# Neighbourhood attention of an encoder block: query tiles by column half, two heads at a time

## The chip, the cores and the metric

The kernel runs on one core of a Trainium2 chip. The metric is the device time of one launch in microseconds; of the kernel before three runs gave 1609.84 to 1613.71, median 1612.07. All inputs and weights are float32 and come from HBM (274.6 MB move in one launch). TensorE's granted clock has two levels here, 2.4 GHz (1.00 in the profile) and 1.2 GHz (0.50).

## The reference, cut to what matters

One encoder layer on 16 meta tokens and 256 tokens (a grid of 4 rows by 64 columns), width 2048. The normalised tokens give q, k, v (16 heads of 64), the input u of a state-space branch and two gates. The part that changes is the attention:

```python
def neighbourhood_attention(q, k, v, rpb):     # rows = 4, kr = min(8, rows) = 4: every grid row is in reach
    col_start = jnp.clip(c_idx - COL_WIN // 2, 0, GRID_W - COL_WIN)          # 16 of 64 columns around the query
    ...
    s_loc = einsum('bchd,bicjhd->bhcij', q_r, k_win) * scale + bias           # 4 rows x 16 columns of keys
    s_meta = einsum('bchd,bmhd->bhcm', q_r, km) * scale                       # and the 16 meta tokens
    p = softmax(concatenate([s_loc, s_meta], axis=-1), axis=-1)
    return einsum(p_loc, v_win) + einsum(p_meta, vm)
```

A query in columns 0 to 31 reaches keys in columns 0 to 39 only, one in columns 32 to 63 keys in columns 24 to 63. Meta queries attend to the meta tokens. Behind it: y_na = attention @ w_proj_na; the state-space branch with GELU and a GLU (w_glu) and w_proj_ssm; both gated, @ w_out, residual; then a gated MLP with a convolution (w_up, w_down) and a last norm.

## The kernel before, in words

**Dense products.** Every weight matrix comes in units of 4 x 128 rows by 256 columns (512 KB) through four ring slots. SyncE's queue loads a unit (`load`, L360); ScalarE rounds it to `w_hi` (`hi_unit`, L426 to L430); GpSimd, in the first stages VectorE, makes the rest `w_lo` (`lo_unit`, L432 to L434); TensorE takes the unit in two halves of 12 matmuls (`half_unit`, L1356 to L1369, three products hi x hi, hi x lo, lo x hi). Each waits for the one before by a counter, and slot and order are fixed: units are always made and used in sequence, and ScalarE can round a unit only when TensorE has used the one four ahead of it.

**Order.** The engines each run their own written-out list; nothing else orders the work. U, V, K, Q and the gates are 16-unit to 64-unit products. V is staged and transposed (`v_blocks`, `v_copy`), K and Q are scaled and staged by VectorE (`kq_block`, L908 to L917), all three are stored to HBM scratch. Beside K run the state-space inputs, beside Q and the first gates its scan on VectorE, and beside two gate blocks its outputs (L1546 to L1567).

**Attention** runs beside the last 8 gate blocks (32 units), one head (index k in loop i) beside two units. The query tile t holds grid rows 2t and 2t+1, all 64 columns, so a head's scores are two tiles of 128 queries by all 272 keys. On TensorE a head is: `scores` (two products, 64 rows of the array, L1600), two units of gate product with `values` of the head before between them (L1621 to L1623, 64 columns of the array), `probs_t` (six transposes, L1608, L1610). float32 products take two instructions each, transposes one. On VectorE `att_scores` (scale, add bias, maximum, negate), `att_norm`, `att_lo`, and a gate block every second head; on ScalarE `att_exp`, one `hi_unit`, every second head `att_hi` and the loads of the next pair (`att_load`, 8 DMA issues), one `hi_unit`, `att_pt` (copies of the transposed probabilities). GpSimd adds a column mask to the loaded bias (L498) for two heads at a time between its `lo_unit` calls; the bias ring has four places, q, k and v rings two.

The state-space branch's GELU stands in ScalarE's list behind the exponentials of the fourth head, and its `gelu_lo` in VectorE's list ahead of the fourth head's `att_norm`. After the last values TensorE waits for the copies, transposes the meta probabilities and starts the GLU; the wait for the last `att_lo` (L1665) stands behind the first GLU product.

## Time and profile before

| | |
|---|---|
| median of 3 runs | 1612.07 us |
| profiled execution | 1610.86 us |
| its span, first to last instruction | 1609.1 us |
| TensorE busy | 1511.4 us (94%) |
| GpSimd busy | 1032.8 us (64%) |
| ScalarE busy | 704.1 us (44%) |
| VectorE busy | 573.6 us (36%) |

Times are microseconds from the span's start unless marked ns. PE is TensorE (PEld its weight loads), DVE VectorE, ACT ScalarE, POOL GpSimd; ACTq is ScalarE's queue, which issues DMAs. Matmuls overlap in the array, so an instruction's duration (0.28 for 258 columns) is longer than the step to the next (0.12): pace is read from starts, not from durations. "idle before" is time in which the engine had nothing to run, with what released it.

### The profile page before, as it was taken

The page shows a single profiled execution, that of the slowest core. Times are in us where ns is not written, and L with a number is a line of the kernel's source. Part 1 is how long each engine was busy: PE and PEld are TensorE (multiplying, and loading weights), DVE is VectorE, ACT ScalarE, POOL GpSimd, SP SyncE. Part 2 cuts the span into 40 slices and gives each one's busy share as a digit, 9 for nine tenths or more (in the row PEclk, how much of TensorE's full clock was granted, in tenths as well). Part 3 has the DMA queues.
Part 4 walks back from the last instruction along what each step waited for, and adds up shares of the span by engine and source line. Part 5 has one row for each costly group of instructions (what it writes and reads, how often), then busy time and mean ns, then how long its engine had stood idle before and what let it go on. Part 6 is the DMA issues. An engine that isn't in the chain of part 4 may idle for free.

```text
span 1609.1 us, 33915 instructions
## 1 busy us (share of the span) xinstructions
PE 1511.4 (94%) x12869; PEld 1462.7 (91%) x12869; DVE 573.6 (36%) x1159; ACT 704.1 (44%) x920; POOL 1032.8 (64%) x461
## 2 busy tenths in 40 slices
PE   6897998977888999999999999999999999999996
PEld 5897998976866888999999999999999999999996
DVE  3564778887534441344232121222121211000002
ACT  4544442320153446444455555555555553333333
POOL 3200026872345565788778888888888887888883
PEclk9899999998988999999999999999999999999998
DMA  5996555652463544557556555655565555555552
GB/s 156 286 204 192 155 157 158 193 155 63 96 157 111 151 142 132 166 182 239 170 157 184 183 182 176 189 182 182 175 190 182 182 176 197 188 183 186 191 183 92
DMA packets 248144, 274.58 MB, mean 171 GB/s; under 512 B 30908, under 2 KB 235100, under 8 KB 247180
## 3 DMA queue, kind: packets, MB, share of 16 engines
q1 hardware_dynamic: 228944, 253.92, 52.1%
q10 hardware_dynamic: 19068, 19.66, 4.3%
q8 instruction: 45, 0.74, 0.2%
q14 instruction: 23, 0.19, 0.0%
q0 software_dynamic: 64, 0.07, 0.0%
HBM read 261.62 MB, written 11.74 MB: 170 GB/s over the span
## 4 chain that ended last, share of the span: by engine, by line
PE 75%; issue 6%; DVE 6%; POOL 4%; DMA 2%; ACT 2%; DVEq 1%; SPq 1%; ACTq 1%; POOLq 0%
PE ps L1365 19%; PE ps L1367 18%; PE ps L1366 18%; PE ps L1709 5%; PE ps L1710 5%; PE ps L1711 5%; POOL w_lo L434 4%; DMA w_raw<-in_w_in 2%; PE ps L1559 1%; DVE ps L931 1%; DVE scan_states L1111 1%; ACT w_hi L430 1%; DVE t L931 1%; DVE w_lo L434 1%; PE ps L1600 1%
## 5 line engine op out<-in xcount | busy, mean ns | idle before, releaser
L434 POOL TENSOR_TENSOR w_lo<-w_raw,w_hi 128x1024 fp32r<-128x1024 f32 x420 | 1010.9, 2417 | 537.6 <-ACT w_hi L430 537.4
L430 ACT ACTIVATE w_hi<-w_raw 128x1024 fp32r<-128x1024 f32 x464 | 488.8, 1059 | 760.2 <-PE ps L1367 513.6
L1365 PE MATMUL ps<-act_hi,w_hi 128*128 128x258 f32 (+2 forms) x2432 | 702.1, 289 | 18.1 <-POOL w_lo L434 9.4
L1367 PE MATMUL ps<-act_hi,w_lo 128*128 128x258 f32 (+2 forms) x2432 | 694.9, 286 | 0.0
L1366 PE MATMUL ps<-act_lo,w_hi 128*128 128x258 f32 (+2 forms) x2432 | 694.1, 285 | 0.0
L1365 PEld LDWEIGHTS ps<-act_hi,w_hi 128*128 128x128 f32 x2432 | 466.1, 192 | 34.0 <-issue 18.6
L1366 PEld LDWEIGHTS ps<-act_lo,w_hi 128*128 128x128 f32 x2432 | 466.9, 192 | 0.0
L1367 PEld LDWEIGHTS ps<-act_hi,w_lo 128*128 128x128 f32 x2432 | 465.1, 191 | 0.0
L1709 PE MATMUL ps<-hidden_hi,w_hi 128*128 (+1 forms) x704 | 197.8, 281 | 2.2 <-DVE gelu_ring L1318 2.2
L1711 PE MATMUL ps<-hidden_hi,w_lo 128*128 (+1 forms) x704 | 197.6, 281 | 0.0
L1710 PE MATMUL ps<-hidden_lo,w_hi 128*128 (+1 forms) x704 | 197.6, 281 | 0.0
L1709 PEld LDWEIGHTS ps<-hidden_hi,w_hi 128*128 128x128 f32 x704 | 133.1, 189 | 2.4 <-DVE gelu_ring L1318 2.4
L1710 PEld LDWEIGHTS ps<-hidden_lo,w_hi 128*128 128x128 f32 x704 | 133.1, 189 | 0.0
L1711 PEld LDWEIGHTS ps<-hidden_hi,w_lo 128*128 128x128 f32 x704 | 133.0, 189 | 0.0
L1331 DVE TENSOR_TENSOR xT<-xT,ps 128x512 f32<-128x512 f32 x8 | 5.0, 682 | 245.2 <-PE ps L1711 245.2
L1314 DVE TENSOR_TENSOR ps<-ps,rstd 128x512 f32<-128x512 f32 x22 | 15.4, 699 | 167.8 <-PE ps L1367 167.8
L434 DVE TENSOR_TENSOR w_lo<-w_raw,w_hi 128x1024 fp32r<-128x1024 f32 x44 | 53.6, 1226 | 56.6 <-ACT w_hi L430 49.4
L1365 PE MATMUL ps<-mixed_hi,w_hi 128*128 128x258 f32 x256 | 73.6, 287 | 0.0
L1367 PE MATMUL ps<-mixed_hi,w_lo 128*128 128x258 f32 x256 | 72.4, 283 | 0.0
L1301 DVE TENSOR_TENSOR ps<-ps,rstd 128x516 f32<-128x516 f32 x22 | 15.5, 703 | 156.8 <-PE ps L1367 156.8
L931 DVE TENSOR_TENSOR ps<-scan_states,ps 64x128 f32<-64x128 f32 (+1 forms) x201 | 59.6, 296 | 6.7 <-issue 0.7
L1365 PEld LDWEIGHTS ps<-mixed_hi,w_hi 128*128 128x128 f32 x256 | 48.4, 189 | 0.2
(242 smaller groups left out, 1618.2 us busy)
## 6 DMA issues: line engine op xcount, KB each, us to landing
w_raw<-in_w_up SPq DMA_DIRECT2D x176, 512.0 KB, 3.5
w_raw<-in_w_in SPq DMA_DIRECT2D x128, 512.0 KB, 3.9
w_raw<-in_w_down SPq DMA_DIRECT2D x88, 512.0 KB, 3.6
w_raw<-in_w_out SPq DMA_DIRECT2D x32, 512.0 KB, 3.6
w_raw<-in_w_proj_na SPq DMA_DIRECT2D x16, 512.0 KB, 3.5
w_raw<-in_w_proj_ssm SPq DMA_DIRECT2D x16, 512.0 KB, 3.5
w_raw<-in_w_glu SPq DMA_DIRECT2D x8, 512.0 KB, 3.4
bias_ring<-skew_scratch ACTq DMA_DIRECT2D x32, 96.0 KB, 3.0
```

The source lines that it names most:

```text
L430: act.activation(slot(whi, k), slot(raw, k), ACT.Copy).then_inc(s_hi, 1)
L434: pool.tensor_tensor(slot(wlo, k), slot(raw, k), slot(whi, k).bitcast(F), ALU.subtract).then_inc(s_lo, 1)
L931: dve.tensor_tensor(o, a, b, ALU.mult)
L1111: dve.tensor_tensor(X[:, c + 1, :], X[:, c + 1, :], prod[:, r, :], ALU.add)
L1365: mm(o, slot(whi, k)[:, cols], xh[:, kt, lo:lo + n], start=kt == 0, stop=False)
L1366: mm(o, slot(whi, k)[:, cols], low, start=False, stop=False)
L1367: ins = mm(o, slot(wlo, k)[:, cols], xh[:, kt, lo:lo + n], start=False, stop=kt == units * UKT - 1)
L1559: mm(o[:, ::-1] if d else o, Gn[:, t % GSLOTS, d, 2 * b + g, :], X[:, 0:NCH, GROUPS * d + TG * t + 2 * b + g], start=d == 0, stop=False, s ...
L1600: ins = mm(ps[:, 2 * hh + t, 0:L], qs[hs, j, 2 + t * P:2 + (t + 1) * P], ks[hs, j, :], start=True, stop=True)
L1709: mm(o, slot(whi, k)[:, cols], xh, start=first and g % 2 == 0, stop=False, skip_group_check=True)
L1710: mm(o, slot(whi, k)[:, cols], xl, start=False, stop=False, skip_group_check=True)
L1711: ins = mm(o, slot(wlo, k)[:, cols], xh, start=False, stop=final, skip_group_check=True)
```

## The change

- Query tile t is now a column half: t = 0 the left 32 columns of all four grid rows, t = 1 the right ones. Each tile has its own list of 160 keys (16 meta, 4 rows x 40 columns), `WK`; the last 32 of them are `NB`. Scores, exponentials and normalisation run on 160 instead of 272 columns.
- K and V are stored to scratch in this order, one copy per half, so the columns that both halves reach are there twice. For that `kq_block` and `v_blocks` copy windows instead of whole blocks, V's scale per key is built in key order (`prs`, four transposes, `tsp`), and `v_copy` has one more copy.
- Both heads of a pair are done in one step b (8 steps instead of 16): `scores` on row halves of the array in turn, `values` on column halves, one VectorE instruction for scale and bias of all four tiles (640 columns), one maximum, which comes out negated. Scores use banks 0 and 1, values their upper columns.
- The values of pair b-1 wait until VectorE has reduced the scores of pair b. The copies of the transposed probabilities move from ScalarE to VectorE, behind the gate block. The gate product uses banks 6, 7 and 2, 3 in turn.
- The bias comes as four loads of 128 runs of 1 KB into one buffer, GpSimd adds the mask into a second buffer, both single; its 4 additions of 160 columns stand behind the third `lo_unit` of the pair before. In ScalarE's list the loads of pair b+1 stand behind `att_hi` of pair b-1, ahead of three `hi_unit` calls.
- The loops of the stage are written out. GELU stands in pair 1, `gelu_lo` in pair 2. 16 mask selections on GpSimd replace 4 and stand behind its first 8 `lo_unit` calls. The wait for the last `att_lo` stands ahead of the first GLU product.

Added lines of the diff (what they replace is in the functions above):

```diff
+QCOLS = GRID_W // 2
+KCOLS = QCOLS + COL_WIN // 2
+KSTEP = GRID_W - KCOLS
+WK = N_META + GRID_ROWS * KCOLS
+NB = WK - P
...
+        def window(tile, h):
+            return tile[:, :, WK * h + N_META:WK * (h + 1)].rearrange("p m (r c) -> p m r c", c=KCOLS)
+        def window_of(tokens, h):
+            return tokens.rearrange("p m (r c) -> p m r c", c=GRID_W)[:, :, :, KSTEP * h:KSTEP * h + KCOLS]
+        def window_source(bank, h):
+            return window_of(ps[:, bank:bank + 2, N_META:L], h)
+        def window_meta(tile):
+            return tile.rearrange("p m (h w) -> p m h w", h=2)[:, :, :, 0:N_META]
+        def window_meta_source(bank):
+            return ps[:, bank:bank + 2, 0:N_META].unsqueeze(2).to_broadcast([P, 2, 2, N_META])
+        def by_query(tokens):
+            return tokens.rearrange("p (r t c) -> p t r c", r=GRID_ROWS, t=2)[:, :, ::-1, :]
...
+            def bias_window(i):
+                pool.wait_ge(s_bl, 64 * (i + 1))
+                if i:
+                    pool.wait_ge(s_nm, i + SEED)
+                for ht in range(4):
+                    hh, t = ht // 2, ht % 2
+                    last = pool.tensor_tensor(
+                        bm[:, ht, N_META:WK].rearrange("p (r w) -> p r w", w=KCOLS),
+                        bi[:, hh, t, :].rearrange("p (r w) -> p r w", w=GRID_W)[:, :, KSTEP * t:KSTEP * t + KCOLS],
+                        mask[:, t, :].unsqueeze(1).to_broadcast([P, GRID_ROWS, KCOLS]), ALU.add)
+                last.then_inc(s_bm, 1)
+            pool.wait_ge(s_bl, 64)
+            pool.memset(bm[:, :, 0:N_META], 0.0).then_inc(s_bz, 1)
+            bias_window(0)
+            for i in range(G_ATT):
+                for n in range(4):
+                    lo_unit(pool, U_G + DEPTH + 4 * (G_SCAN + G_SSM + i), n)
+                    if n == 2 and i + 1 < G_ATT:
+                        bias_window(i + 1)
...
+                for h in range(2):
+                    act.activation(vst[:, h, :], ps[:, b, h * CB:(h + 1) * CB], ACT.Copy, scale=tsp[:, h:h + 1])
+                    act.activation(vst[0:NB, 2 + h, :], ps[0:NB, b + 1, h * CB:(h + 1) * CB], ACT.Copy,
+                                   scale=tsp[0:NB, 2 + h:3 + h])
...
+                    act.activation(window_meta(stg[:, k, :, :]), window_meta_source(2 * k), ACT.Copy)
+                    for h in range(2):
+                        last = act.activation(window(stg[:, k, :, :], h), window_source(2 * k, h), ACT.Copy)
+                    last.then_inc(s_vtd, 1)
...
+            def att_load(b):
+                j = b % 2
+                act.dma_start(qs[:, j, :], q_d[b, :, :]).then_inc(s_qkv[j], 16)
+                act.dma_start(ks[:, j, :], k_d[b, :, :]).then_inc(s_qkv[j], 16)
+                act.dma_start(va[:, j, :, :],
+                              v_d[:, 0:P, b * P:(b + 1) * P].rearrange("h p c -> p h c")).then_inc(s_qkv[j], 16)
+                act.dma_start(vb[0:NB, j, :, :],
+                              v_d[:, P:WK, b * P:(b + 1) * P].rearrange("h p c -> p h c")).then_inc(s_qkv[j], 16)
+                if b:
+                    act.wait_ge(s_bm, b)
                 for hh in range(2):
+                    for t in range(2):
+                        rows = skew_d[QCOLS * t:QCOLS * (t + 1), DROWS * (2 * b + hh):DROWS * (2 * b + hh) + GRID_ROWS, :]
+                        by_row = bass.AP(rows.tensor, rows.offset, [[GRID_W, GRID_ROWS], [HEADS * DROWS * GRID_W, QCOLS],
+                                                                    [1, GRID_ROWS * GRID_W]])
+                        act.dma_start(bi[:, hh, t, :], by_row).then_inc(s_bl, 16)
+            def att_exp(b):
+                act.wait_ge(s_nm, b + 1 + SEED)
+                for ht in range(4):
+                    last = act.activation(S[:, ht, :], S[:, ht, :], ACT.Exp,
+                                          bias=stat[:, 0, ht:ht + 1], accum_out=stat[:, 1, ht:ht + 1])
+                last.then_inc(s_e, 1)
+            def att_hi(b):
+                act.wait_ge(s_pv, b + 1 + SEED)
                 for t in range(2):
+                    last = act.activation(by_query(anh[:, b, 2:NL])[:, t, :, :],
+                                          ps[:, t, 2 * WK:2 * WK + P].rearrange("p (r c) -> p r c", c=QCOLS), ACT.Copy)
+                last.then_inc(s_ah, 1)
...
+            for b in range(G_ATT):
+                att_exp(b)
+                hi_unit(act, att_u + DEPTH, 4 * b)
+                if b:
+                    att_hi(b - 1)
+                if b + 1 < G_ATT:
+                    att_load(b + 1)
+                for n in range(1, 4):
+                    hi_unit(act, att_u + DEPTH, 4 * b + n)
+                    if b == 1 and n == 1:
+                        y_gelu()
+            att_hi(G_ATT - 1)
...
+                if n < 4:
+                    by_meta = rstd[:, 0:N_META].unsqueeze(1).unsqueeze(1).to_broadcast([P, 2, 2, N_META])
+                    dve.tensor_tensor(window_meta(stg[:, n % 2, :, :]), window_meta_source(banks), by_meta, ALU.mult)
+                    for h in range(2):
+                        by = window_of(rstd[:, N_META:L].unsqueeze(1).to_broadcast([P, 2, SEQ]), h)
+                        dve.tensor_tensor(window(stg[:, n % 2, :, :], h), window_source(banks, h), by, ALU.mult)
+                else:
+                    for m in range(2):
+                        dve.tensor_tensor(stg[:, n % 2, m, 0:SEQ].rearrange("p (t r c) -> p t r c", t=2, c=QCOLS),
+                                          by_query(ps[:, banks + m, 2:NL]), by_query(rstd[:, N_META:L]), ALU.mult)
...
+            dve.tensor_copy(prs[0:1, :].rearrange("p (h w) -> p h w", h=2)[:, :, 0:N_META],
+                            rstd[0:1, 0:N_META].unsqueeze(1).to_broadcast([1, 2, N_META]))
+            for h in range(2):
+                dve.tensor_copy(window(prs[0:1, :].unsqueeze(1), h), window_of(rstd[0:1, N_META:L].unsqueeze(1), h))
...
+            def att_scores(b):
+                dve.wait_ge(s_qk, b + 1)
+                dve.wait_ge(s_bm, b + 1)
+                dve.wait_ge(s_bz, 1)
+                if b:
+                    dve.wait_ge(s_ptps, b)
+                dve.scalar_tensor_tensor(
+                    out=S[:, :, :].rearrange("p (h t) w -> p h (t w)", h=2), in0=ps[:, 0:2, 0:2 * WK], scalar=SCALE,
+                    in1=bm[:, :, :].rearrange("p (h t) w -> p h (t w)", h=2), op0=ALU.mult, op1=ALU.add)
+                dve.drain()
+                dve.reduce_max(stat[:, 0, :], S[:, :, :], AX.X, negate=True).then_inc(s_nm, 1)
+            def att_norm(b):
+                dve.wait_ge(s_e, b + 1)
+                dve.reciprocal(stat[:, 1, :], stat[:, 1, :])
+                dve.drain()
+                for ht in range(4):
+                    last = dve.tensor_scalar(S[:, ht, :], S[:, ht, :], stat[:, 1, ht:ht + 1], None, ALU.mult)
+                last.then_inc(s_p, 1)
+            def att_pt(b):
+                dve.wait_ge(s_ptps, b + 1)
+                if b:
+                    dve.wait_ge(s_pv, b + SEED)
+                dve.tensor_copy(PA[:, :], ps[:, 4, :])
+                dve.tensor_copy(PB2[0:NB, :], ps[0:NB, 5, :]).then_inc(s_ptsb, 1)
+            def att_lo(b):
+                dve.wait_ge(s_ah, b + 1)
                 for t in range(2):
+                    last = dve.tensor_tensor(by_query(anl[:, b, 2:NL])[:, t, :, :],
+                                             ps[:, t, 2 * WK:2 * WK + P].rearrange("p (r c) -> p r c", c=QCOLS),
+                                             by_query(anh[:, b, 2:NL].bitcast(F))[:, t, :, :], ALU.subtract)
+                last.then_inc(s_al, 1)
+            att_u = U_G + 4 * (G_SCAN + G_SSM)
+            for b in range(G_ATT):
+                att_scores(b)
+                att_norm(b)
+                if b:
+                    att_lo(b - 1)
+                if b == 2:
+                    dve.wait_ge(s_ygh, 1)
+                    dve.tensor_tensor(ygl[:, :, :], yT[:, :, LIVE:L], ygh[:, :, :].bitcast(F), ALU.subtract).then_inc(s_ygl, 1)
+                if b == G_ATT - 1:
+                    att_pt(b)
+                dve.wait_ge(s_used, att_u + 4 * (b + 1))
+                gate_block(gate_ssm, 2 * b, (6, 2)[b % 2])
+                if b < G_ATT - 1:
+                    att_pt(b)
+            att_lo(G_ATT - 1)
...
+            for h in range(2):
+                nc.tensor.transpose(ps[:, 5, 4 * FT + h:4 * FT + h + 1], prs[0:1, WK * h:WK * h + P], ident[0:1, 0:1])
+                nc.tensor.transpose(ps[0:NB, 5, 4 * FT + 2 + h:4 * FT + 3 + h], prs[0:1, WK * h + P:WK * (h + 1)],
+                                    ident[0:1, 0:1])
...
+            def scores(b):
+                j = b % 2
+                pe.wait_ge(s_qkv[j], 64 * (b // 2 + 1))
+                if b > 1:
+                    pe.wait_ge(s_al, b - 1 + SEED)
                 for t in range(2):
+                    for hh in range(2):
+                        hs = slice(DH * hh, DH * (hh + 1))
+                        ins = mm(ps[:, hh, WK * t:WK * (t + 1)], qs[hs, j, t * P:(t + 1) * P],
+                                 ks[hs, j, WK * t:WK * (t + 1)], start=True, stop=True)
                 ins.then_inc(s_qk, 1)
+            def probs_t(b):
+                pe.wait_ge(s_p, b + 1)
+                if b:
+                    pe.wait_ge(s_ptsb, b)
+                for ht in range(4):
+                    nc.tensor.transpose(ps[:, 4, P * ht:P * (ht + 1)], S[:, ht, 0:P], ident[:, :])
+                    ins = nc.tensor.transpose(ps[0:NB, 5, P * ht:P * (ht + 1)], S[:, ht, P:WK], ident[:, :])
+                ins.then_inc(s_ptps, 1)
+            def values(b):
+                j = b % 2
+                pe.wait_ge(s_ptsb, b + 1)
+                pe.wait_ge(s_nm, min(b + 2, G_ATT) + SEED)
                 for t in range(2):
+                    for part in range(2):
+                        for hh in range(2):
+                            hs = slice(DH * hh, DH * (hh + 1))
+                            col = slice(P * (2 * hh + t), P * (2 * hh + t + 1))
+                            o = ps[hs, t, 2 * WK:2 * WK + P]
+                            if part == 0:
+                                mm(o, va[:, j, t, hs], PA[:, col], start=True, stop=False, skip_group_check=True)
+                            else:
+                                ins = mm(o, vb[0:NB, j, t, hs], PB2[0:NB, col], start=False, stop=True,
+                                         skip_group_check=True)
+                ins.then_inc(s_pv, 1)
+            att_u = U_G + 4 * (G_SCAN + G_SSM)
+            for b in range(G_ATT):
+                if b:
+                    scores(b)
+                pe.wait_ge(s_g, G_SCAN + G_SSM + b - 1 + SEED if b else G_SCAN + G_SSM + SEED)
+                for n in range(4):
+                    if b == G_ATT - 1 and n == 3:
+                        probs_t(b)
+                    for m in range(2):
+                        half_unit(att_u, 4 * b + n, n, 4, m, hnh, hnl, LIVE, NL, (6, 2)[b % 2] + m)
+                    if n == 0 and b:
+                        values(b - 1)
+                    elif n == 0:
+                        scores(b)
+                if b < G_ATT - 1:
+                    probs_t(b)
+            values(G_ATT - 1)
...
+            pe.wait_ge(s_g, 16 + SEED)
...
+            pe.wait_ge(s_al, KH + SEED)
```

## Rows read from the trace of the kernel before

**Rows 1.** Windows: length; busy us (instructions) of PE, PEld, DVE, ACT, POOL; clock; DMA.

```profile
432.10:610.70 178.60, 159.91 (x1032) 129.77 (x1026) 70.86 (x150) 75.55 (x142) 94.95 (x49) 0.92 0.53 140
488.80:499.00 10.20, 10.19 (x39) 8.02 (x40) 3.09 (x9) 4.31 (x8) 1.76 (x2) 0.56 0.25 77
532.00:607.50 75.50, 75.50 (x512) 61.74 (x512) 30.69 (x73) 33.02 (x70) 45.71 (x24) 1.00 0.48 143
```

**Rows 2.** Waits of TensorE: line, releaser, us in total, times, longest.

```profile
PE ps L1608 <- DVE scores L1203: 16.2, 2, 11.4
PE ps L1546 <- DVE gate_na L899: 13.6, 1, 13.6
...
PE ps L1455 <- ACT qkv_stage L640: 6.3, 1, 6.3
```

**Rows 3.** Timeline of TensorE, one head: start, length of the merged run, what.

```profile
569.12 0.38 PE L1608 MATMUL ps<-ident,scores 128*128 128x128 f32 x2
...
569.87 1.18 PE L1600 MATMUL ps<-k_ring,q_ring 64*128 64x272 f32 x4
570.98 0.39 PE L1365 MATMUL ps<-act_hi,w_hi 128*128 128x258 f32 x1
571.21 0.28 PE L1366 MATMUL ps<-act_lo,w_hi 128*128 128x258 f32 x1
...
573.82 0.28 PE L1367 MATMUL ps<-act_hi,w_lo 128*128 128x258 f32 x1
574.03 0.65 PE L1621 MATMUL ps<-probs_t,v_ring 128*64 128x256 f32 x2
...
575.61 0.39 PE L1365 MATMUL ps<-act_hi,w_hi 128*128 128x258 f32 x1
...
579.33 1.18 PE L1600 MATMUL ps<-k_ring,q_ring 64*128 64x272 f32 x4
```

**Rows 4.** Timeline of TensorE: products on row halves, and on four column strips.

```profile
160.34 2.00 PE L1499 MATMUL ps<-u_chunks,w_tr 64*128 64x68 f32 x32 [1.90 <-ACT w_tr L661]
...
375.02 0.64 PE L1546 MATMUL ps<-g_nat,b_states 128*32 128x128 f32 x16
```

**Rows 5.** Timeline of ScalarE's queue: loads of one pair, first and last.

```profile
576.05 0.35 ACTq L707 DMA_DIRECT2D q_ring<-q_scratch  x1
...
577.91 2.44 ACTq L715 DMA_DIRECT2D bias_ring<-skew_scratch  x4
```

**Rows 6.** The page, DMA issues: count, KB each, us to landing.

```profile
bias_ring<-skew_scratch ACTq DMA_DIRECT2D x32, 96.0 KB, 3.0
```

**Rows 7.** Groups of instructions, 434 to 610: busy us, mean ns, idle before.

```profile
L434 POOL TENSOR_TENSOR w_lo<-w_raw,w_hi 128x1024 fp32r<-128x1024 f32 x33 | 79.5, 2412 | 81.3 <-ACT w_hi L430 81.3
...
L430 ACT ACTIVATE w_hi<-w_raw 128x1024 fp32r<-128x1024 f32 x32 | 33.5, 1052 | 43.3 <-issue 22.3 <-PE ps L1367 21.0
...
L722 ACT ACTIVATE scores<-scores,att_stats 128x272 f32<-128x272 f32 x32 | 16.4, 514 | 45.8 <-DVE att_stats L1196 45.8
L498 POOL TENSOR_TENSOR bias_ring<-bias_ring,col_mask 128x384 f32<-128x384 f32 x16 | 15.8, 1007 | 6.5 <-DMA bias_ring<-skew_scratch 6.5
...
L1189 DVE SCALAR_TENSOR_TENSOR scores<-ps,bias_ring 128x256 f32<-128x256 f32 x32 | 12.1, 419 | 45.0 <-POOL bias_ring L498 23.4 <-PE ps L1600 21.4 <-issue 0.2
...
L1194 DVE TENSOR_REDUCE att_stats<-scores 128x2 f32<-128x544 f32 x16 | 11.5, 719 | 1.2
```

**Rows 8.** Timeline of GpSimd: the second bias mask of the stage.

```profile
441.92 0.99 POOL L498 TENSOR_TENSOR bias_ring<-bias_ring,col_mask 128x384 f32<-128x384 f32 x1 [2.18 <-DMA bias_ring<-skew_scratch]
```

**Rows 9.** Timeline of ScalarE: GELU of the state-space branch.

```profile
474.34 1.28 ACT L765 ACT_TABLE_LOAD   x1
...
479.78 1.92 ACT L767 ACTIVATE gelu_hi<-y_ssm 128x2064 fp32r<-128x2064 f32 x1
```

**Rows 10.** Timeline of ScalarE: copies of one V block.

```profile
148.54 0.83 ACT L623 ACTIVATE v_stage<-ps,token_stats 128x256 f32<-128x256 f32 x2
```

**Rows 11.** Source line L914 of VectorE: ns min/median/max, first and last start.

```profile
L914 DVE TENSOR_TENSOR qkv_stage<-ps,rstd x8: 695/706/725, 169.8 to 287.4; 128x544 f32<-128x544 f32 x4, 128x516 f32<-128x516 f32 x4
```

More of the change, by code:

```diff
@@ L276, in encoder_block @@
         s_qkv = [sem(f"qkv_loaded_{i}") for i in range(2)]
-        s_bl = [sem(f"bias_loaded_{i}") for i in range(4)]
+        s_bl = sem("bias_loaded")
+        s_bz = sem("meta_bias_zeroed")
         s_bm = sem("bias_masked")
@@ L512, in _ @@
         def _(act):
-            for seeded in (s_ptsb, s_ge, s_vtd, s_vcp):
+            for seeded in (s_ge, s_vtd, s_vcp):
                 act.sem_inc(seeded, SEED)
@@ L1351, in _ @@
         def _(pe):
-            for seeded in (s_pv, s_sq_used, s_vtp, s_ptps):
+            for seeded in (s_pv, s_sq_used, s_vtp):
                 pe.sem_inc(seeded, SEED)
```

241 lines of the change are left out of this document (47 added, 194 removed).

## The prediction, made before the kernel was run

> **What bounds the kernel now.** I read the views from coarse to fine. The windows come first: the attention stage, nearly all that the change rebuilds, runs from its first dense matmul at 432.1 to the end of its last values at 610.7, 178.6 us with TensorE busy for 159.9 of them [rows 1]. From 532 to 607.5 us TensorE is busy without a break at the full clock, VectorE 41% and GpSimd 61% [rows 1]: the even part of the stage is TensorE's. Earlier, from 488.8 to 499, it worked at a granted clock of 0.56, nearly all at the lower level of 1.2 GHz [rows 1]. The waits name the holes ahead of that: the transposes of the probabilities waited 16.2 us in two waits for the normalised scores, the longest 11.4 [rows 2]. Two waits outside also matter, since work is added ahead of them: 6.3 us for the staged V block, 13.6 us for the scan on VectorE [rows 2].
>
> One head in TensorE's timeline [rows 3]: from scores to scores is 579.33 - 569.87 = 9.46 us, a pair of heads 18.92. Dense matmuls start every (573.82 - 571.21)/22 = 0.119 us; 96 of them are 11.4 us a pair. The other 7.5 us a pair are attention. Per head: transposes 0.75 (569.12 to 569.87), scores 1.11 plus 0.11 because the first dense matmul behind them takes 0.23 instead of 0.12, values 1.67 (573.82 + 0.12 to 575.61) plus 0.10 in the same way. Of the stage's 178.6 us 16 x 9.46 = 151.4 are this, and 27 holes and half clock.
>
> **TensorE per pair after.** Scores: 8 instructions as before, but of 160 instead of 272 columns, and the two heads on row halves, alternately. Now one takes (1.18 - 0.39 + 0.10)/4 = about 0.23 for 272 columns [rows 3], 0.84 ns a column, so 0.135 for 160. Do halves overlap? 32 instructions on alternating row halves, 68 columns each, took 2.00 us, 0.0625 each, with 128 columns of weights to load; alone a stream of 68 columns is 0.057 and its weights would come on top, so the halves do overlap. 16 instructions of 128 columns on four column strips took 0.64 less the last one's 0.27, that is a step of about 0.11 per four [rows 4]. So scores are 4 x 0.135 = 0.54, with the change of array shape in front (0.11) and behind (0.2) 0.85. Transposes: 8 instead of 12, at 0.109: 0.87, and 0.1 of shape change. Values: 16 instructions of 128 columns on column halves, 8 x 0.109 = 0.87. Now values take 1.58 from first to next dense (574.03 to 575.61) for six streams of 256 columns, 0.215 each by the same 0.84 ns a column; with 0.1 on each side that leaves 0.48 for three shape changes, 0.16 each. After, values change shape five times (full height and 32 rows in turn for both query tiles), 0.8. Sum 0.97 + 0.85 + 1.67 = 3.5 us; with the dense part 14.9 us a pair against 18.9. If TensorE went on setting the pace, 8 pairs would give 32 us.
>
> The Trainium skill ("TensorE: Matmul & The Clock Gate", Part 3) says that weight loads overlap with matmuls in flight only where the row group differs, which speaks against column halves. The 0.11 per four strips [rows 4], the bare stream, disagrees for this shape. By the rule the values would be serial, 16 x 0.109 = 1.74, and the pair 15.8.
>
> **What is late next.** With TensorE 4 us shorter a cycle through the other engines shows. In the new code the values of pair b-1 wait until VectorE has read the scores of pair b (negated maximum ready, call it M). From M: values 1.67 and signals about 0.3; only then may ScalarE's queue pass the wait in front of the attention output and issue the 8 loads of pair b+1. Eight such issues took 4.3 us now (576.05 to 577.91 + 2.44 = 580.35) [rows 5], and they lay beside exponentials and a split; behind the wait they hold back the splits (hi parts) of units 1 to 3. Then hi of unit 1 ends 1.15 later [rows 7], GpSimd's lo of units 1 and 2 are 2 x 2.41, the four mask additions of pair b+1 stand behind them in its order, and VectorE needs these for the next scores. A mask addition of 384 columns is 1.01 and a split of 1024 2.41 [rows 7], so 2.2 ns a column: 160 columns 0.51, four 2.05. VectorE: 256 columns with bias 0.42, 544 columns reduced 0.72 [rows 7]; 640 columns I take at 0.85 each, 1.8 with signals. Cycle: 2.0 + 4.3 + 1.15 + 0.1 + 4.8 + 2.05 + 1.8 = 16.2 us. It is longer than TensorE's 14.9, so TensorE idles about 1.3 us a pair in front of the values, too little for its clock. ScalarE's four exponentials (0.51 for 272 columns [rows 7], about 0.45 each) lie beside the issues and cost nothing; without that cover they would add 1.8.
>
> Not shown in the trace is an issue of the new bias load: 128 runs of 1 KB instead of 64 of 1.5 KB. Between the q load's 0.35 and the old bias load's 0.61, and up to 0.9 if it grows with the runs, four cost 1.4 to 3.6; I take 2.44, the nearest row. Ends of the cycle: 15.1 and 17.4. A load lands about 3 us behind its issue [rows 6]; the masks stand 6 us behind the last issue because of the splits, so the landing has 3 us to spare.
>
> **The stage.** Begin: the last bias load of pair 0 landed at about 441.9, where GpSimd's second mask started [rows 8]. All four are awaited now: masks until 444.2, M(0) = 446.0. TensorE gets through its units and idles 3 to 4 us, as before (4.8). For pair 0 there are no values in the cycle: M(1) = 446.0 + 14.2 = 460.3. Pair 1 has the GELU of the state-space branch (with its table load and the copy behind it 474.34 to 481.70 [rows 9]) between hi 1 and hi 2: it lengthens the cycle by 7.3 + 1.1 - 2.4 = 6, M(2) = 460.3 + 16.2 + 6 = 482.5. Then five cycles: M(7) = 563.5. Behind it values 1.8, two units 5.7, transposes 1.0, the last unit 2.9, values 1.7: 576.5. Half clock: TensorE idles about 4, 5 and 7 us ahead of pairs 1 to 3; now the 11.4 us hole was followed by 10.2 us at 0.56, some 4 us lost [rows 1, 2]. Most of that falls into the next wait; I add 3. End 579.5 against 610.7: -31. Behind it the first GLU product waits for the last attention lo (0.5 + 0.6 + signals), which was later in the order: +1.3.
>
> **Ahead of the stage.** V: each block is staged in 3 copies instead of 1 and copied out in 5 instead of 4. A 256-column copy is about 0.36 from start to start, and the last two blocks stand in a line with their stores [rows 10] ahead of the first scan product (TensorE is already late there [rows 2]): 2 x 0.36 + 0.25, with the larger store +1.2. K: VectorE's one product of 544 columns, 0.71 [rows 11], becomes 64 + 2 x 320 columns, about 1.05: 4 x 0.35 = 1.4. VectorE has gaps in that stage, I take 0.5. Q: two products of 256 for one of 516, +0.1 x 4 = 0.4, all of it on the way to the scan's end, for which TensorE waits 13.6 us. Parameters: three copies on one partition and four tiny transposes, +0.6. The 16 mask selections on GpSimd that replace 4 come behind its first eight splits, and what waits for the table they hold back is only the SP queue ahead of the K loads, two products later; I cost them at nothing, and at their whole length if the table came late. Together +2.7; 1 to 5.
>
> **Sum.** -31 + 1.3 + 2.7 = -27. The profiled execution took 1610.86 (span 1609.1), so 1584; the median of the runs, 1612.07, is 1.2 above it, I forecast 1584.5.
>
> **Rivals.**
> - TensorE stays the bound. The written-out loads have fixed addresses; if the bias issues take 0.35, the cycle is 15.1. For it: q and k take 0.35 to 0.45. Against: the bias load has two levels of stride. Six cycles of 1.1: 1578.
> - The cycle is longer: bias issues at 0.9, or mask additions slower on the strided window. +1.2 for seven cycles: 1593.
> - The halves do not overlap, in both shapes: TensorE 14.9 + 0.54 + 0.87 = 16.3 a pair, level with the cycle; with half clock 1588. Rows 4 speak against it. (The rule of the Trainium skill above would be this rival for the values alone.)
> - Slower than before: the bias loads land late. They are issued after the values of the pair before and single-buffered; masks, scores and then the values of the pair before stand behind them. The spare is 3 us behind a landing of about 3; the end is on the slower side when each landing costs 3.9 us more than that spare, about 10 us. Then the cycle is 20.1 and the gain of 27 is used up; at 12 us 1625. For it: at the begin GpSimd waited 2.18 us more for the second bias load behind the first [rows 8]. Against: the engines' share later is 0.48 [rows 1].
>
> **How the numbers follow.** Forecast (cycle 16.2, 1577 to 1592 with the begin and the half clock) 0.50; TensorE the bound 0.18; longer cycle 0.21; no overlap 0.06; late loads 0.05. The 8-in-10 range takes the first three with their bounds: 1573 to 1600. Less than 0.2% is what cannot be told from no change here, 3.2 us. Faster 0.95, within 0.01, slower 0.04.
>
> **What would show it.** Of after: 0.11 between pairs of values instructions and 0.135 between pairs of scores; TensorE's wait in front of the values on VectorE's reduction, about 1.3 us a pair, and 16.2 us from pair to pair; ScalarE's 4.3 us of issues behind the values; the 11.4 us wait gone, 5 and 7 us in front of the values of pairs 0 and 1. Wrong, if the pairs follow at 14.9 (issues cheap), or if GpSimd's masks wait for loads instead of for the splits.

## The result, and the profile after

The changed kernel takes 1618.91 us (median of 20 runs), the kernel before 1610.29 (20 runs beside it): ratio 1.0045, 95% interval 1.0036 to 1.0054. It is slower by 0.45%; forecast were 1584.5 us and 0.95 for faster. The profiled execution took 1621.31, span 1619.6, which is 10.5 longer than the span before.

One number of the text above has to be set right first. The key list of a column half is 16 meta keys plus a window of 4 x 40 = 160 grid keys: WK is 176 and the tail NB 48, not 160 and 32. The rows below show it: 64x176, 128x704, 48x512.

TensorE's waits in the changed kernel (total us, times, longest), which answer to [rows 2]:

```profile
PE ps L1672 <- DVE att_stats L1235: 22.6, 7, 5.7
PE ps L1595 <- DVE gate_na L930: 13.6, 1, 13.6
PE ps L1657 <- DVE scores L1242: 12.4, 1, 12.4
...
PE ps L1504 <- ACT qkv_stage L681: 6.2, 1, 6.2
...
PE ps L1548 <- ACT w_tr L703: 3.8, 1, 3.8
```

The waits of 16.2 us for the normalised scores became 12.4, but 22.6 us in seven waits are new: in front of the values of every pair but the last, for VectorE's maximum of the next pair. The same stretches as in [rows 1], by windows (us; busy time and count of PE, PEld, DVE, ACT, POOL; granted clock; DMA share; GB/s): the stage, and its even part.

```profile
442.90:617.20 174.30, 137.75 (x1030) 124.02 (x1027) 49.78 (x101) 60.01 (x116) 92.45 (x66) 0.85 0.56 151
524.00:601.60 77.60, 66.23 (x513) 60.21 (x512) 22.65 (x50) 25.20 (x57) 47.44 (x33) 0.91 0.55 162
```

TensorE's work in the stage fell from 159.9 to 137.8 us, much as meant. The stage is only 4.3 us shorter (174.3 against 178.6), since TensorE is idle for 36.6 us of it and its clock is 0.85 on average. The stage also begins 10.8 us later (442.9 against 432.1).

One cycle, pair to pair. TensorE's timeline shows how fast it now is where nothing holds it (start, duration, ..., count, idle before and what ended it):

```profile
563.02 0.44 PE L1672 MATMUL ps<-probs_t,v_ring 128*64 128x128 f32 x4 [1.45 <-DVE att_stats L1235]
563.39 0.44 PE L1674 MATMUL ps<-probs_t_tail,v_tail_ring 48*64 48x128 f32 x4
563.75 0.45 PE L1672 MATMUL ps<-probs_t,v_ring 128*64 128x128 f32 x4
564.13 0.69 PE L1674 MATMUL ps<-probs_t_tail,v_tail_ring 48*64 48x128 f32 x4
564.75 0.58 PE L1410 MATMUL ps<-act_hi,w_hi 128*128 128x258 f32 x1
...
574.67 0.27 PE L1657 MATMUL ps<-ident,scores 128*128 128x128 f32 x1
...
575.64 0.87 PE L1648 MATMUL ps<-k_ring,q_ring 64*128 64x176 f32 x8
576.43 0.38 PE L1410 MATMUL ps<-act_hi,w_hi 128*128 128x258 f32 x1
...
579.27 0.28 PE L1412 MATMUL ps<-act_hi,w_lo 128*128 128x258 f32 x1
582.34 0.44 PE L1672 MATMUL ps<-probs_t,v_ring 128*64 128x128 f32 x4 [2.79 <-DVE att_stats L1235]
```

Values 1.73 us, transposes 0.97, scores 0.79. The halves do overlap: at the prediction's 0.84 ns a column, eight score instructions of 176 columns in a row would take 1.18 us, and a group of four values instructions, 0.37 from start to start here, 0.43. The clock halves within these values, as the 0.69 at 564.13 shows; at the full clock they take 1.47 (experiment 6). But from 579.55 to 582.34 nothing runs. What was late stands in the timelines of ScalarE with its queue, of GpSimd and of VectorE:

```profile
564.88 0.32 ACTq L749 DMA_DIRECT2D q_ring<-q_scratch  x1
...
566.73 2.25 ACTq L762 DMA_DIRECT2D bias_rows<-skew_scratch  x4
569.20 1.06 ACT L457 ACTIVATE w_hi<-w_raw 128x1024 fp32r<-128x1024 f32 x1 [3.21 <-PE ps L1412]
```

```profile
573.20 2.40 POOL L461 TENSOR_TENSOR w_lo<-w_raw,w_hi 128x1024 fp32r<-128x1024 f32 x1 [0.46 <-ACT w_hi L457]
578.28 1.97 POOL L528 TENSOR_TENSOR bias_window<-bias_rows,col_mask 128x160 f32<-128x160 f32 x4 [2.68 <-DMA bias_rows<-skew_scratch]
```

```profile
580.34 0.89 DVE L1231 SCALAR_TENSOR_TENSOR scores<-ps,bias_window 128x704 f32<-128x704 f32 x1 [3.31 <-issue]
581.31 0.89 DVE L1235 TENSOR_REDUCE att_stats<-scores 128x4 f32<-128x704 f32 x1
```

The chain closes: values at 563.02, last bias issue over at 568.98 (5.96), data at 578.28 (9.30), masks until 580.25 (1.97), VectorE and its signal until the next values at 582.34 (2.09). Sum 19.32, which is the period, and longer than the 18.92 of a pair before [rows 3]. Of the forecast's terms all but the landing hold: it was to be 3. GpSimd had ended its splits at 575.60, 6.6 us behind the last issue (forecast 6), and waited the other 2.7 of the 9.3 for the data.

What the DMA engines did in such a landing, in a stretch of the pair before (share of the 16 engines by queue; q1 is SP's, weights, q10 ScalarE's, here bias alone):

```profile
DMA packets 234, 0.23 MB, mean 97 GB/s; under 512 B 6, under 2 KB 234, under 8 KB 234
...
q1 hardware_dynamic: 125, 0.12, 15.2%
q10 hardware_dynamic: 109, 0.11, 13.0%
```

From 553.6 to 556.0 us two loads were in flight, and all engines together were busy for 28% of their time: 4.5 of 16, at 22 GB/s each. The bias load's pattern has 4 grid rows outermost. That the load runs on few engines is read from this share here, and shown by experiments 3 and 4. The weight load seems to be caught as well, with its rest on the same few engines: over the stage weights land 5.1 us behind their issue, where it was 3.8 in the stage before and is 4.0 in that of experiment 3. An estimate of the landing's size: the 512 KB of four bias loads take 6 us on four engines at 22 GB/s each, counted from the first issue at 566.73; shared with the weight loads they took until 578.28.

### The profile page after: what moved, and what is told of

It reads as the page before. It is cut to its first block, busy times and chain, and to the rows that moved or that the text cites. A ratio compares the mean times of both kernels' runs of the same rounds, so it can differ in the third digit from the quotient of the medians.

```text
span 1619.6 us, 33652 instructions
## 1 busy us (share of the span) xinstructions
PE 1503.6 (93%) x12881; PEld 1470.3 (91%) x12881; DVE 555.3 (34%) x1128; ACT 690.8 (43%) x907; POOL 1039.0 (64%) x490
## 4 chain that ended last, share of the span: by engine, by line
PE 71%; DVE 10%; DMA 6%; issue 4%; ACT 3%; DVEq 2%; ACTq 1%; SPq 1%; POOL 1%
PE ps L1410 17%; PE ps L1412 17%; PE ps L1411 17%; PE ps L1756 5%; PE ps L1758 5%; PE ps L1757 5%; DMA bias_rows<-skew_scratch 4%; DVE ps L969 3%; DVE scan_states L1155 2%; DMA w_raw<-in_w_in 2%; DVEq L1154 1%; PE ps L1608 1%; ACT w_hi L457 1%; ACTq L762 1%; DVE t L969 1%
## 5 line engine op out<-in xcount | busy, mean ns | idle before, releaser
L1410 PE MATMUL ps<-act_hi,w_hi 128*128 128x258 f32 (+2 forms) x2432 | 706.8, 291 | 16.2 <-POOL w_lo L461 9.3
L1410 PEld LDWEIGHTS ps<-act_hi,w_hi 128*128 128x128 f32 x2432 | 472.3, 194 | 23.7 <-issue 12.0
L1411 PEld LDWEIGHTS ps<-act_lo,w_hi 128*128 128x128 f32 x2432 | 472.9, 194 | 0.0
L1412 PEld LDWEIGHTS ps<-act_hi,w_lo 128*128 128x128 f32 x2432 | 470.6, 193 | 0.0
L1359 DVE TENSOR_TENSOR ps<-ps,rstd 128x512 f32<-128x512 f32 x22 | 15.4, 700 | 167.9 <-PE ps L1412 167.9
```

The source lines that it names most:

```text
L1410: mm(o, slot(whi, k)[:, cols], xh[:, kt, lo:lo + n], start=kt == 0, stop=False)
L1411: mm(o, slot(whi, k)[:, cols], low, start=False, stop=False)
L1412: ins = mm(o, slot(wlo, k)[:, cols], xh[:, kt, lo:lo + n], start=False, stop=kt == units * UKT - 1)
```

## Experiments

Every time is a median beside runs of the kernel before on the same chip, but for three single runs in experiment 4; the ratio with its interval is to those.

**1. Loads earlier.** Bias loads of pair b+1 ahead of the exponentials of pair b:

```
 for b in range(G_ATT):
+    if b + 1 < G_ATT:
+        bias_load(b + 1)        # waits s_bm b+1, four issues
     att_exp(b)
     ...
-        att_load(b + 1)         # q, k, v, bias
+        att_load(b + 1)         # q, k, v
```

> The changed kernel with one edit: the four bias loads of pair b+1 are issued ahead of the exponentials of pair b (as soon as GpSimd has masked pair b), no longer behind the attention output of pair b-1. The q, k and v loads stay. Theory (late loads): in the changed kernel the cycle from values to values is 5.96 us to the end of the last bias issue, 9.3 us until it lands, 2.0 of masks and 2.1 of VectorE, together 19.3. Issued 6 us earlier, the loads land ahead of the masks' turn, the cycle becomes TensorE's own 15.05 (16.4 us of its work in that cycle less 1.3 lost at half clock). Six cycles of about 4 and one hole of 5.5 give 25 to 30 us: 1589 to 1594, GpSimd's wait for bias rows 0 for the pairs behind the first, TensorE's waits in front of the values under 5 us instead of 22.6. Rival (TensorE is slower than worked out, because the halves or the shape changes themselves cost the clock): the cycle only falls to 17 or more, under 15 us gained, 1604 or more, with half clock in every pair though the holes are gone. Rival (the loads only take the memory's bandwidth): they land as late, 1616 or more.

Measured 1596.99, ratio 0.9904 (0.9878 to 0.9930): 22 us less than the changed kernel, short of the 25 to 30. GpSimd's waits for bias rows fell from 12.6 us to 0.6 and the cycle was 15.12 us in two pairs. In one of the even pairs it was 20.97, for a reason not foreseen: q, k and v now stand behind the slow bias load in the same queue. TensorE waited 3.5 us at 547.10 for the tail of V, whose issue had ended at 537.2, and then worked at a clock of 0.57 for 6 us. The longest such wait, 4.5 us, stands at the start of the stage, where experiment 3 has one of 5.8 too; it doesn't belong to the few engines. TensorE's waits in the stage:

```profile
PE ps L1662 <- DVE scores L1247: 13.7, 1, 13.7
PE ps L1653 <- DMA v_tail_ring<-v_scratch: 10.1, 4, 4.5
PE ps L1677 <- DVE att_stats L1240: 6.0, 2, 5.5
```

**2. The wait that closes the cycle, taken out.** The sums move to other banks, so that no wait is needed there:

```
 def values(b):
     pe.wait_ge(s_ptsb, b + 1)
-    pe.wait_ge(s_nm, min(b + 2, G_ATT) + SEED)
...
-    o = ps[hs, t, 2 * WK:2 * WK + P]
+    o = ps[hs, 4 + t, 0:P]
 # probs_t(b) waits s_al, b + SEED
```

> The changed kernel with the values' sums moved from the banks of the scores to the banks of the transposed probabilities, which are free by then: the values of pair b-1 no longer wait for VectorE's maximum of pair b. The bias loads stay behind the attention output. Theory (late loads close a cycle through that wait): the loads still land 9.3 us behind their issue, but what they hold back is now only the probabilities of the next pair, needed 25.3 us after the values where they are ready after 23.3. TensorE sets the pace, 15.05 us a pair: 1589 to 1594, waits in front of the values gone, GpSimd still waits for bias rows in most pairs. Rival (the landing alone sets the pace, through GpSimd's order): the splits behind the masks hold TensorE's dense products, cycle 17 to 18, 1600 to 1610, TensorE waiting for the splits L461.

Measured 1601.68, ratio 0.9948 (0.9928 to 0.9967). The theory's 1589 to 1594 was missed. Cycles of 16.6 to 18.1 us behind the pair with the GELU: the rival, which gave 17 to 18 and 1600 to 1610. GpSimd waits for bias rows 15.9 us in six waits instead of 12.6, and the split behind the masks in its order then holds a dense product:

```profile
PE ps L1646 <- DMA v_tail_ring<-v_scratch: 6.8, 7, 1.2
PE ps L1656 <- DVE attn_lo L1255: 6.0, 6, 5.0
PE ps L1410 <- POOL w_lo L461: 3.8, 5, 1.1
```

So the wait was the way by which the landing reached TensorE, and 17 us hung on it; the landing is as late without it and still costs.

**3. The same load over all engines.** Bias loads where they were, by grid row, 32 columns outermost. The scratch becomes [column of the half, head, half, row, width], so that two heads by two halves are one dimension of 4:

```
-for hh in range(2):
-    for t in range(2):
-        # source [4 rows][32 columns][1 KB]
-        act.dma_start(bi[:, hh, t, :], by_row)
+for r in range(GRID_ROWS):
+    # source [32 columns][4 = head x half][1 KB]
+    act.dma_start(bi[QCOLS * r:QCOLS * (r + 1), :, :, :], by_column)
```

> The changed kernel, the bias loads where they were, four issues of 128 KB a pair as before, but each now takes one grid row (32 partitions, outermost in the pattern, by 4 runs of 1 KB) instead of all four grid rows of one head and half (outermost dimension 4). For that the scratch is laid out with the two halves of a column pair behind each other. Theory: with four entries in the outermost dimension only 4 of the 16 DMA engines carry the load; behind its issues the DMA share falls to 0.28 with 97 GB/s. Spread over 32, the last load lands 3 us behind its issue instead of 9.3, the cycle through it is 13.1, and TensorE sets the pace at 15.05 us: 1585 to 1592, waits in front of the values under 6 us together, GpSimd waits for bias rows only for pair 0. Rival (what counts is the bytes, 512 KB a pair instead of 384, or the queue they stand in): landing stays over 8 us, 1615 to 1619.

Measured 1582.71, ratio 0.9817 (0.9796 to 0.9839): 36 us less than the changed kernel with the same bytes in the same place of the same queue. (Each load also writes 32 partitions with 4 KB instead of 128 with 1 KB; experiment 4 leaves the written side as it is.) The stage, and three cycles of its even part:

```profile
435.30:580.00 144.70, 125.87 (x1027) 114.53 (x1028) 49.77 (x101) 59.89 (x116) 92.31 (x66) 0.93 0.75 182
521.20:567.40 46.20, 45.06 (x386) 41.22 (x387) 16.18 (x36) 18.75 (x43) 34.46 (x25) 1.00 0.76 204
```

The page gives the loads 4.1 us from the start of an issue to its landing. While they are under way (542.5 to 544.5 us) ScalarE's queue keeps 70% of the engines' time busy, where it was 13%, and all queues move 220 GB/s, where they moved 97. GpSimd goes from its split at 547.83 straight to the masks, with no wait:

```profile
bias_rows<-skew_scratch ACTq DMA_DIRECT2D x32, 128.0 KB, 4.1
```

```profile
q10 hardware_dynamic: 400, 0.36, 69.6%
```

```profile
543.11 4.72 POOL L462 TENSOR_TENSOR w_lo<-w_raw,w_hi 128x1024 fp32r<-128x1024 f32 x2 [1.43 <-ACT w_hi L458]
547.80 1.97 POOL L529 TENSOR_TENSOR bias_window<-bias_rows,col_mask 128x160 f32<-128x160 f32 x4
```

Pairs follow at 15.36 to 15.49 us, with waits of 0.3 to 0.4 in front of the values. This is the kernel that the prediction described. Stage 144.7 us against 147.4 forecast; whole 1582.7 against 1584.5. That it comes so near is partly luck: the first values start 30.8 us into the stage instead of 28.2, the six cycles behind them take 101.3 us together instead of 103.2, and the 3 us added for the half clock aren't needed.

Not all of the 36 us are the landing. The stage begins 7.6 us earlier in this profile (435.3 against 442.9), which has the short hole of experiment 5 without an edit for it; the windows give the stage itself 29.6.

**4. The number of entries outermost, alone, in the kernel before.** Same 64 runs of 1.5 KB, same addresses, another order (n = 2, 4, 8, 16 for 64):

```
-act.dma_start(bi[...], skew_d[:, ds(row, EWIN), :])
+act.dma_start(bi[...], skew_d[:, ds(row, EWIN), :].rearrange("(m n) r w -> n m (r w)", n=n))
```

> The kernel before the change, its 32 bias loads of 96 KB with the same 64 runs of 1.5 KB from the same addresses, but in an order whose outermost dimension has 2 entries (and 32 within) instead of 64. The rows of the bias come permuted, so the result isn't the reference's. Theory (the outermost dimension is what is spread over the DMA engines, each at some 22 GB/s as in the changed kernel's 97 GB/s at a share of 0.28): four loads in a row take 2.2 us each on two engines, median landing 6 to 8 us instead of 3.0. Rival (the pattern doesn't matter, the larger load did): 3.0.

> As outer_2 with 4 entries outermost (16 within). Theory: four loads in a row at 1.1 us each on four engines, median landing 4 to 5 us. GpSimd's masks stand behind the loads in the kernel before as well, but two heads later: time within 2 us of before. Rival: landing 3.0.

> As outer_2 with 8 entries outermost. Theory: 0.55 us each, hidden by the issues 0.6 apart: landing 3.0 to 3.5 us.

> As outer_2 with 16 entries outermost. Both: 3.0 us, as with 64.

GpSimd's waits for its bias rows in this kernel, for 16, 8, 4 and 2 entries (total, times, longest); with 64 the group of [rows 7] has 6.5:

```profile
POOL bias_ring L498 <- DMA bias_ring<-skew_scratch: 7.2, 2, 4.7
```

```profile
POOL bias_ring L498 <- DMA bias_ring<-skew_scratch: 10.5, 2, 6.6
```

```profile
POOL bias_ring L498 <- DMA bias_ring<-skew_scratch: 13.6, 2, 9.5
```

```profile
POOL bias_ring L498 <- DMA bias_ring<-skew_scratch: 19.3, 5, 11.6
```

Monotone, from 16 to 2 by a factor of 2.7. Besides the order only the issues changed a little (median 0.51 us with 64, 0.57, 0.61, 0.55 and 0.53 with 16, 8, 4 and 2). How many engines the bias loads keep busy is read from the share of ScalarE's queue in the 1 us behind the last group of issues, again for 16, 8, 4 and 2 (from 581, 586, 587 and 589 us):

```profile
q10 hardware_dynamic: 125, 0.15, 81.0%
```

```profile
q10 hardware_dynamic: 85, 0.12, 41.2%
```

```profile
q10 hardware_dynamic: 67, 0.10, 26.3%
```

```profile
q10 hardware_dynamic: 30, 0.05, 12.3%
```

8, 4 and 2 engines of 16 would be 50, 25 and 12.5%: under 16 the number of busy engines follows the count of the outermost dimension, and the 28% of the changed kernel, for both queues together, are about its four. For 16 the page gives a landing of 3.3 us (3.0 with 64); for 8, 4 and 2 it gives none. In this last group the queue's packets end about 12 us behind the last issue with 2 entries, 5 with 4, and 2 to 3 with 8 and 16: there 8 are as good as 16, as expected. The waits of GpSimd are longer because they stand elsewhere: with 16, 8 and 4 entries, as with 64, both are at the start of the stage, where the loads of the scan's output are in flight too. Later the masks of the kernel before stand far enough behind the loads, and only 2 entries give three more waits (0.2 to 0.6 us). What the few engines cost in even pairs is shown by experiment 3, not here.

At the start, then, 4 entries cost the kernel before 5 us: 1617.34, ratio 1.0032 (1.0014 to 1.0049), where within 2 us was expected. TensorE's wait for the normalised scores grew from 16.2 to 21.5 us. The others are single runs: 1614.18 (16), 1619.29 (8), 1622.00 (2).

The Trainium skill ("DMA: Bandwidth & Descriptors", Rules for kernel authors, and the section on why a DMA increments its semaphore by 16) says that the slowest dimension of the patterns sets the number of engines, the largest divisor of both sides up to 16, and warns of an outermost dimension under 16. The row of 28% and experiments 3 and 4 (12, 26 and 41% for 2, 4 and 8 entries) agree. The prediction could have used it and did not.

**5. Ahead of the stage.** The V block staged and stored as before:

```
-# 3 copies into stg, 16 transposes, 5 copies out, stores of 2 x 128 and 2 x 48 rows
+# 1 copy of 544 columns, 8 + 4 transposes, 4 copies out, stores of 256 and 16 rows
```

> The changed kernel with the V block staged and stored as before the change: one copy of 544 columns instead of three, 8 + 4 transposes instead of 16, four copies out instead of five, a store of 256 KB and one of 16 KB a block instead of two larger ones; the attention then reads other rows of V, so what it computes isn't attention over the right tokens, while its loads have the same size. Theory: of the 7.7 us by which the scan starts later than the common shift of the start, 2.3 come from the V tail (2 x 0.36 of copies, 1.4 longer wait for the store) and 4.1 from the half clock behind the hole of 3.8 us that it makes; with the old staging both go: 1611 to 1614 (-5 to -8). Rival (the products of K and Q on windows cost it): no more than 1.5 us gained, 1617 or more.

and, for itself, the wait for the V stores a little later:

```
-act.wait_ge(s_vst, 16 * 8)
-act.wait_ge(s_pd, 1)
 hi_unit(act, U_K + DEPTH, 0)
 wt_copy(0)
 hi_unit(act, U_K + DEPTH, 1)
+act.wait_ge(s_vst, 16 * 8)
+act.wait_ge(s_pd, 1)
```

> The changed kernel with ScalarE's (and VectorE's) wait for the V stores moved from in front of the first split and the first weight copy of the K stage to behind them, in front of the first write into the memory that the stores read. Theory: TensorE waited 3.8 us for that copy and then worked 10 us at the lower clock, which cost 4.1 more. Without the hole 6 to 8 us are gained: 1611 to 1613, the granted clock of the 10 us behind it is 1.00. Rival (the scan on VectorE sets the end of the stage, whatever TensorE does in its beginning): TensorE's wait for the scan grows from 13.6 us by what is gained, 1618 to 1620.

Measured 1612.33, ratio 1.0009 (0.9993 to 1.0026), and 1612.98, ratio 1.0016 (1.0000 to 1.0031): 6.6 and 5.9 us less than the changed kernel, as expected. The first 10 us of the K stage, in the changed kernel (ahead of them TensorE waited 3.8 us for the weight copy) and with the later wait (no such wait), by windows with the columns as above:

```profile
166.50:176.50 10.00, 10.00 (x66) 9.88 (x67) 6.29 (x9) 3.27 (x5) 0.00 (x0) 0.58 0.54 147
```

```profile
160.70:170.70 10.00, 10.00 (x107) 9.78 (x108) 7.72 (x11) 5.35 (x7) 0.00 (x0) 1.00 0.49 132
```

66 against 107 products in the same 10 us, at 0.58 of the clock: about 4 us are lost to it, more than the hole grew (1.9 to 3.8). ScalarE's wait for the store was 5.0 us in the changed kernel, 3.5 before. It varies between profiles with the same V code: 2.9 in experiment 2 (hole 2.8, clock 0.83 behind it) and 2.8 in experiment 3 (hole 0.9, clock 1.00). What makes the store land later in one than in another wasn't settled.

**6. Together.** Experiment 3 with the later wait:

> The kernel bias_spread with the wait for the V stores moved behind the first weight copy (as in v_wait_later, which gained 5.9 us). The two edits lie in different stages, so they should add: 5 to 7 us less than bias_spread, 1579 to 1586. Rival: the earlier scan is given back in front of the attention (pair 0 waits for its bias): under 2 us.

Measured 1579.85, ratio 0.9800 (0.9775 to 0.9825): 2.9 us less than experiment 3, between theory and rival, but with intervals that overlap widely, so it isn't clear of the noise. The hole in front of the K stage is 0.9 us in both profiles, so there was little to gain. With the values in the other banks as well:

> The kernel spread_v with the values' sums in the banks of the transposed probabilities (as in values_free). Theory: with the loads in time VectorE's maximum comes level with TensorE's need, so nothing of size is left to gain: within 2 us of spread_v, or 1 to 3 slower where the transposes now wait for the attention's low part (6.0 us in six waits in values_free, five of that in the pair with the GELU). Rival (the wait for the maximum still costs 1 us or more in each pair): 4 to 8 us less than spread_v.

Measured 1575.42, ratio 0.9777 (0.9757 to 0.9797). 4.4 us less, with intervals that overlap a little: the rival's size, not the theory's, but not by the rival's way, which wanted 1 us or more in each pair. The steady pairs follow at 15.01 instead of 15.37 us, four of them 1.4 us, now with TensorE alone as the bound; the two cycles around the GELU take 34.9 instead of 38.8 us, where spread_v has a wait of 6.4 us in front of the values. One steady pair:

```profile
542.96 0.44 PE L1672 MATMUL ps<-probs_t,v_ring 128*64 128x128 f32 x4
...
557.97 0.44 PE L1672 MATMUL ps<-probs_t,v_ring 128*64 128x128 f32 x4
```

This is the fastest of the kernels tried, 2.2% under the kernel before. Last, experiment 3 with the later wait, and the scan's output loaded and put through the GELU later:

```
-    load_in(U_G, 4 * HALF, 4, range(6)); y loads; load_in(U_G, 4 * HALF, 4, range(6, 8))
+    load_in(U_G, 4 * HALF, 4); load_in(U_G, 4 * HALF, 5, range(2)); y loads; ...
-    if b == 1 and n == 1: y_gelu()
+    if b == 2 and n == 1: y_gelu()
```

> The kernel spread_v with the eight loads of the scan's output (SP's queue, 15.4 us of issues in the changed kernel, 445.3 to 460.8) three weight loads later, and the GELU and its split one pair later. Theory: the bias of pair 0 shares the DMA engines with these and lands at 462, 14 us behind its last issue, which makes the 12.4 us wait of the first transposes; without them beside it, it lands by 452 and 4 to 7 us are gained on spread_v. Rival (the spread load passes them anyway, or the same time is lost where the GELU now stands): within 2 us of spread_v.

Measured 1588.65, ratio 0.9849 (0.9825 to 0.9872): 8.8 us worse than without. The first values did come 4.0 us sooner (461.6 against 465.6), but the next cycles took 21.7, 23.6 and 18.3 us against 21.4, 17.4 and 15.4. The rival had named that place, without the size. Spreading alone had already cured about half of pair 0: GpSimd's wait for its rows 16.9 to 8.0 us, the eight issues of the scan's output 15.37 to 8.21.

## Why the prediction was wrong

The step that failed is the sentence "A load lands about 3 us behind its issue [rows 6]". Rows 6 are of a load of 96 KB with 64 entries outermost; it was carried over to one of 128 KB with 4. I had noticed the new shape, but bounded only its issue (1.4 to 3.6; it took 2.25). The landing took 9.3. In the sum it stood at nothing, hidden by 6 us of splits. The cycle became 3.9 us longer than with the spread load (19.3 against 15.4): 2.7 are GpSimd's wait above, the rest is the half clock behind the holes, which delays the products that release the splits (masks ready to start 12.6 us behind the values instead of 11.3).

- **TensorE per pair**: right. 14.9 forecast, 15.01 measured where nothing else bounds it. Values at the full clock 1.47, or 1.64 with the longer steps at both ends that the forecast counts (1.67), transposes 0.97 (0.97), scores 0.79 (0.85), in spite of the key list being 176 long. The overlap of the halves, for which there were only [rows 4], held; 16 values instructions in a row would have been 1.74 for themselves and the pair 15.8.
- **The cycle**: mechanism right, and named exactly: values behind the maximum, loads behind the values. Eight issues 4.10 (4.3), masks 1.97 (2.05), VectorE 0.89 twice (0.85). With the spread load it ran at 15.4 instead of 16.2: from the values' start the last issue was over after 5.4 us instead of 6.3 (1.6 to the first issue for 2.0, 3.8 for the eight instead of 4.3), and VectorE with its signals took 2.1 instead of 1.8.
- **The rival "bias loads land late"** is what happened. Its price was right: it put a cycle of 20.1 at a landing of 10 us, the point where the gain is used up, and the kernel has 9.3 and 19.3, plus a worse start. Its chance of 0.05 was too low. It had been weighed by the engines' mean share (0.48 [rows 1]), and by nothing about the load's own pattern. Here too the mean share is only 0.55, and 0.28 in the landing above. A low share was read as room, where it can mean that a load has few engines.
- **Start of the stage**: forecast holes of 5 and 7 us, found 12.4, 5.7 and 5.5. The bias of pair 0 landed at 462, 14 us behind its issue, with the scan's output in flight beside it.
- **Half clock**: I added 3 us. In the stage it came back behind six of the seven waits in front of values (1.45 to 5.66 us), and not behind that of 1.18, after which the clock stayed at 1.00. A hole of 1.3, as forecast, had been called too little for the clock; it lies between these two. Behind the 1.45 us at 563.02 (windows, as above):

```profile
564.70:567.40 2.70, 2.70 (x14) 2.65 (x13) 1.64 (x7) 1.28 (x4) 1.66 (x1) 0.50 0.85 235
```

- **Ahead of the stage**: forecast 2.7, range 1 to 5. The two edits of experiment 5 show 6 to 7 us from the V tail alone. Its copies were counted; missed was that a hole growing from 1.9 to 3.8 us takes the clock with it. In their profiles the scan of the kernels with the mended tail comes at most 1.7 us behind the kernel before, counted from the same point of the start; so K, Q and parameters cost at most that, near the forecast. About 3 of the 10.8 us lie in the first 50 us and vary from profile to profile by as much (the same products, with the scale diagonals, start at 43.8 to 47.8).

- **Behind the stage**: forecast 1.3. From the stage's end to the last instruction it is 1002.4 us against 998.4, 4.0 more. The wait for the attention's low part is there (0.6 us); not in the sum was the clock in the 7.8 us behind the stage's end, in the changed kernel and before:

```profile
617.20:625.00 7.80, 7.21 (x61) 7.11 (x60) 0.49 (x2) 1.70 (x4) 2.96 (x2) 0.78 0.39 129
```

```profile
610.70:618.50 7.80, 7.53 (x97) 7.27 (x96) 0.43 (x2) 2.79 (x5) 2.46 (x3) 1.00 0.21 69
```

The account, in spans: forecast 1582.1 (1609.1 - 27), measured 1619.6, 37.5 too little; in the medians 34.4, mainly since the profiled execution lies 2.4 above its median. 26.9 are the stage (174.3 for 147.4): 29.6 for the landing (174.3 - 144.7), less the 2.7 by which the stage without it is shorter than forecast. 8.1 lie ahead of the stage (10.8 for 2.7), about 6 of them the V tail with its clock. 2.7 lie behind it (4.0 for 1.3).

## What to carry to other kernels

When a DMA's pattern changes, price its landing anew and not only its issue and bytes: look at the count of the outermost dimension first, then at the DMA share in the stretch of the landing, where a small steady share with several loads in flight means few engines. Where a recurrence runs through a load (issue behind a result, result behind the load), each microsecond of its landing is paid once per turn; write the cycle as a sum and ask which term no row of the kernel has shown with this shape. An added copy in front of a short hole costs more than itself where the hole then takes TensorE's clock down.

## What was not expected of the hardware

- A slow load on few engines delays other loads, of its own queue and of SP's: TensorE waited 3.5 us for V in an even pair of experiment 1, and weight loads took 5.1 us over the stage, 4.0 with the spread load.
- 2, 4 and 8 entries outermost kept 12, 26 and 41% of the engines' time busy (experiment 4).
- Four entries outermost instead of 64 cost even the kernel before 5 us, through the first of its 32 loads of 96 KB.
- TensorE's hole ahead of the K stage and the granted clock of the 10 us behind it, over five profiles: 0.9 and 1.00, 1.9 and 1.00, 2.8 and 0.83, 3.2 and 0.72, 3.8 and 0.58.
